# Two products of the scans, made as two products of 64 columns of weights where there was one of 128

## The reference, cut to what matters

```python
def step(S, inp):
    r_t, w_t, kk_t, a_t, v_t, k_t = inp
    sa = jnp.einsum('dbhij,dbhj->dbhi', S, -kk_t)
    S = S * w_t[..., None, :] + sa[..., None] * (kk_t * a_t)[..., None, :] + v_t[..., None] * k_t[..., None, :]
    return S, jnp.einsum('dbhij,dbhj->dbhi', S, r_t)
```

## Time and profile before

| | us |
|---|---|
| median of 3 runs | 3783.78 (3783.37 to 3785.37) |
| the profiled execution, its own time | 3779.27 |
| its span, first to last instruction | 3777.6 |
| scans stage, first to last chunk's work on PE | about 1058 to 1920 |
| one chunk in the middle of the stage | 24.0 |

### The profile page before, as it was taken

The page is one execution under the profiler, slowest core; times in us unless marked ns, Lnnn a source line. Parts: engine busy times, 40 slices in busy tenths (PEclk is TensorE's granted clock), DMA queues, the critical chain, the costliest instruction groups (busy, mean ns, idle before and its releaser), DMA issues. The chain is left out here.

```text
span 3777.6 us, 91654 instructions
## 1 busy us (share of the span) xinstructions
PE 3246.2 (86%) x37497; PEld 2921.0 (77%) x37497; DVE 2299.3 (61%) x4531; ACT 1613.9 (43%) x2876; POOL 852.2 (23%) x1205
## 2 busy tenths in 40 slices
PE   5879989998958999999948981699999999999990
PEld 2867776667658999999947770699999999999990
DVE  2555458985546777777757768355555555555542
ACT  2312665554633444444435640344444444444432
POOL 0100000000045666666622200111211111211001
PEclk8989999999878999999979985799999999999995
DMA  5444335654442444444366631555665555665536
GB/s 177 125 150 163 87 95 171 197 178 147 145 125 69 98 99 98 101 101 100 82 165 190 186 111 56 192 180 179 189 193 181 187 178 174 200 189 179 180 112 206
DMA packets 583699, 560.27 MB, mean 148 GB/s; under 512 B 212001, under 2 KB 527841, under 8 KB 582413
## 3 DMA queue, kind: packets, MB, share of 16 engines
q1 hardware_dynamic: 550768, 458.43, 40.9%
q0 software_dynamic: 32608, 97.26, 9.1%
HBM read 418.30 MB, written 137.27 MB: 147 GB/s over the span
## 5 line engine op out<-in xcount | busy, mean ns | idle before, releaser
L3114 DVE TENSOR_TENSOR exp_wlo<-exp_raw,exp_whi 128x2048 fp32r<-128x2048 f32 x192 | 440.5, 2294 | 373.8 <-ACT exp_whi L3067 373.8
L3067 ACT CAST exp_whi<-exp_raw 128x2048 fp32r<-128x2048 f32 x192 | 365.6, 1904 | 96.0 <-DMA exp_raw<-in_w_gate 96.0
L954 PE MATMUL mix_acc<-proj_hThi,mix_wlo 128*128 128x448 f32 (+3 forms) x920 | 366.2, 398 | 14.4 <-DVE mix_wlo L1279 14.4
L954 PE MATMUL mix_acc<-proj_hTlo,mix_whi 128*128 128x448 f32 (+3 forms) x920 | 342.7, 372 | 0.0
L954 PE MATMUL mix_acc<-proj_hThi,mix_whi 128*128 128x448 f32 (+3 forms) x920 | 342.3, 372 | 0.0
L3002 PE MATMUL exp_g<-exp_xThi,exp_wlo 128*128 128x272 f32 x1024 | 299.0, 292 | 8.6 <-DVE exp_xTlo L3118 7.4
L3002 PE MATMUL exp_o<-exp_hidhi,exp_wlo 128*128 128x272 f32 x1024 | 305.3, 298 | 0.0
L3002 PE MATMUL exp_g<-exp_xThi,exp_whi 128*128 128x272 f32 x1024 | 297.2, 290 | 0.0
L3002 PE MATMUL exp_o<-exp_hidhi,exp_whi 128*128 128x272 f32 x1024 | 296.7, 290 | 0.0
L3002 PE MATMUL exp_u<-exp_xThi,exp_wlo 128*128 128x272 f32 x1024 | 296.6, 290 | 0.0
L3002 PE MATMUL exp_u<-exp_xThi,exp_whi 128*128 128x272 f32 x1024 | 296.3, 289 | 0.0
(11 more groups left out here) (366 smaller groups left out, 8631.8 us busy)
## 6 DMA issues: line engine op xcount, KB each, us to landing
exp_raw<-in_w_gate SPq DMA_DIRECT2D x64, 1024.0 KB, 5.2
exp_raw<-in_w_up SPq DMA_DIRECT2D x64, 1024.0 KB, 5.2
exp_raw<-in_w_down SPq DMA_DIRECT2D x64, 1024.0 KB, 5.2
scn_plain<-rec SPq DMA_DIRECT2D x68, 384.0 KB, 3.6
rec<-mix_arena SPq DMA_DIRECT2D x24, 896.0 KB, 4.3
proj<-mix_out POOLq DMA_DIRECT2D x88, 224.0 KB, 2.6
scn_grc<-grec SPq DMA_DIRECT2D x136, 128.0 KB, 3.9
mix_arena<-in_w_ada SPq DMA_DIRECT2D x12, 1024.0 KB, 5.8
```

Source lines behind the costliest of these rows:

```text
L954: mm = pe.matmul(acc[n % ACCS][0:width, 0:tn], wt[:, k, 0:width], hT[hp][:, k, t0:t0 + tn], start=k == 0 and i == 0, stop=k == KD - 1 and ...
L3067: act.copy(w[k % RING][0][:, :, :], raw[k % RAW][:, :, :]).then_inc(hi_done[k % RING], 1)
L3114: dve.tensor_tensor(w[k % RING][1][:, :, :], raw[k % RAW][:, :, :], w[k % RING][0][:, :, :], ALU.subtract).then_inc(lo_done[k % RING], 1)
```

## The change

`read_out` and `keys_by_token` make each product of 128 columns of weights as two of 64 columns: the first takes columns 2C:3C and writes the low 64 partitions of the output, the second takes columns 3C:4C and writes the high 64. What is moved past them (the readings, or the identity `eye`) is the same for both. The same numbers land at the same places; the waits and semaphores are as before.

```diff
                         for h, p in enumerate(HALVES):
-                            mm = pe.matmul(cols(pRK[g][h], x, C), plain[u][p, j, 2 * C:4 * C], plain[u][p, j, C:2 * C], start=True, stop=True)
+                            for half, keys in ((LOW, slice(2 * C, 3 * C)), (HIGH, slice(3 * C, 4 * C))):
+                                mm = pe.matmul(cols(pRK[g][h], x, C)[half], plain[u][p, j, keys], plain[u][p, j, C:2 * C], start=True, stop=True)
...
                             for h, p in enumerate(HALVES):
-                                mm = pe.matmul(cols(pBK[g][h], x, C), plain[u][p, j, 2 * C:4 * C], eye[p], start=True, stop=True)
+                                for half, keys in ((LOW, slice(2 * C, 3 * C)), (HIGH, slice(3 * C, 4 * C))):
+                                    mm = pe.matmul(cols(pBK[g][h], x, C)[half], plain[u][p, j, keys], eye[p], start=True, stop=True)
```

## The result

The changed kernel takes 3792.39 us (median of 11 runs, 3782.22 to 3798.19), the kernel before 3782.54 (11 runs, 3776.01 to 3786.37). The ratio is 1.0025, with a 95% interval of 1.0014 to 1.0036: some 9.5 us slower, where 73 us less was forecast. The execution that was profiled is the changed kernel's quickest, 3782.22 us, so its trace shows less of the loss than the median has.

What follows compares the result with a forecast made beforehand. PE's own sequence was taken to bound each chunk: 3.55 us removed less 1.40 added gives 2.15 us, 73 us over 34 chunks, so 3783.8 - 73 = 3711 us, range 3704 to 3766.

Steps and rivals of the forecast that it cites:

- What bounds the kernel: In each chunk PE's own sequence sets the time, apart from one loop through DVE of 0.9 us.
- 2.15: Gain in us per chunk: 3.55 removed (products and borders) less 1.40 added; 73 us over 34 chunks.
- The price of the new products: The 48 products of 64 x 64 a chunk run four at once, 0.029 us each, 1.40 us; chance 0.47.
- 2.80 us: Rival: only two positions work at once, so the 48 products cost 2.80 us; 25 us faster, 3759; chance 0.32.
- The borders: Changes of form around the three changed groups cost 0.29 us each, 0.87 us a chunk, and would go to zero.
- The step that failed: Issue of 24 more products a chunk costs nothing, hidden while PE's queue is ahead of its array.
- 0.0583: Time in us of a 64 x 64 product before, the best rate of any group, read as two positions at once.
- DVE: It all but sets the stretch after the last changed group, which moves with that group, neither longer nor shorter.
- wait of 0.94 us: PE's one long wait for DVE, between 1519.77 and 1534.57 us, should stay.
- The rival on the other side: Switching output halves on the same rows costs 0.05 us a start, 4.00 us for 48; 15 us slower, 3799; chance 0.11.
- likeliest case: Four positions at once: 73 us faster, 3711 us, own range 3704 to 3728; chance 0.47.

Runs made afterwards that it cites:

- after_t: Kernel before with keys_by_token as one-pass transposes of 64 x 128 and read_out split into 64-column halves: 3760.52 us, ratio 0.9958.
- positions: Kernel before plus a stage ahead with PE alone on f32 products: 1600 round four positions 89.0 us, 1600 in two 93.6, 800 with 128 columns 89.3.
- experiments 8 and 9: Changed kernel and kernel before, each with most scan loads cut to one row from the fourth chunk: 3767.38 us (0.9966) and 3777.31 us (0.9993).

## Why the prediction was wrong

**What bounds the kernel** was half right. The claim was that PE's own sequence sets a chunk. PE's sequence is two things, the array and the supply of its instructions, and the kernel before was close to the limit of both. The instruction queue of 1300 to 1500 us, before and then changed:

```profile
q8 instruction: 44, 0.72, 1.6%
```

```profile
q8 instruction: 46, 0.75, 1.6%
```

That is a portion every 4.55 us before and every 4.35 now. In the changed kernel the waits in this stage follow each other at 256 instructions (125 or 126 product records, as many loads and the waits for semaphores), most of them 4.1 to 5.1 us apart (3.6 to 5.6, median 4.4), two or three in a row; then some 500 records, four portions, mostly pass in about 17 us, 4.2 to 4.3 each, without one. The supply, not the array, sets its chunk. Counted in the traces, a chunk of the kernel before is 5.26 portions and one of the changed kernel 5.64. At 4.35 us a portion, the pace of the changed kernel, a chunk before would need 22.9 of its 24.1 us: an estimate, by which about 1.2 us a chunk, not 2.15, was there to be had by anything that leaves the count alone. And the change didn't leave it alone. The pace is read off the changed kernel itself; what supports it is another kernel with another count: the chunks of `after_t`, 5.36 portions in 23.52 us, go at 4.39.

**The price of the new products** was nearly right: 1.40 us for 48. By starts, the steps behind those of 1962 and 1974 took 47.3 us in 29.5 chunks, 1.60 a chunk, where the old ones took 92.7 in 29.8, 3.11. Four positions do work at once, also where two share their rows. The rule of the Trainium skill's TensorE: Matmul & The Clock Gate (packing small matmuls), by which 2.80 us was worked out, isn't borne out here, and that of the Trainium skill's TensorEngine Tiling (Array Packing), Tiling Modes, is: 0.029 us a product in the bursts of `positions`. **The borders** vanished: the neighbour at 1509.60 is at 0.70.

**The step that failed** is "I cost the new issue of 24 more products at nothing: it is hidden as long as PE's queue is ahead of its array", and with it "the products would be paid at the rate of issue, which isn't slower than the 0.0583 seen". First, the queue isn't ahead: its supply is what the faster array runs into. Second, 0.0583 was no bound on the supply. It was seen where slower products, 64 x 128 at 0.112 us, stood between and let the portions catch up (64 of them last 7.2 us). Beside the traffic of the scans the waits that follow at one portion's distance are 4.4 us apart at the median, 0.069 us for an f32 product. The change took these slow products out and put more instructions in. 24 more products are 96 instructions, 0.375 of a portion, 1.6 us at 4.35. So of the 2.15 us a chunk that the array was to give, about 1.2 could be had at that pace, and the new instructions need 1.6. The chunk went from 24.09 to 24.52, with the four spells of half the clock in it.

**DVE** was judged rightly in that it wasn't what stopped the gain: its waits fell from 20.1 to 5.7 us. The prediction wanted its wait of 0.94 us, one of these, to stay. That they shrank because PE came later is likely, and wasn't tested. The reading of the trace of before that would have warned isn't in the one chunk of the earlier trace rows, which has no wait of PE for issue. It is in the list for 1100 to 1850: 8.1 us in 11 pieces, of which 3.8 are the piece behind `scn_SX` and 4.3 are short waits, each at a multiple of 256 instructions. In so full a stretch, an engine that waits for nothing visible was here the sign of a supply at its edge.

**The rival on the other side** had the right sign and nearly the right size (15 us slower, 9.5 measured), but by luck: its mechanism was a start of 0.05 us at each switch of halves, and in `positions` bursts round four positions run at 0.029 us. (A slip without weight: by its own terms the upper end of the likeliest case is 3730, not 3728.)

**Open.** That a portion waits for a transfer is shown by the count of instructions, the packets' size and their times. With PE alone its distance of 3.46 us is made up of 1.0 to 1.2 us until the next packet starts, 0.9 to 1.1 of the packet and 1.2 to 1.5 until its instructions are used; what the first and the last of these are spent on isn't shown. Of the 3.6 to 5.6 us in the scans, the traffic explains a part (experiments 8 and 9); the rest was not taken apart. What brings the clock to half behind some waits and not behind others as long isn't shown. The trace of the changed kernel is of its quickest run; of the runs that took 10 us more there is none.

## What to carry to other kernels

Before making matmuls shorter, count the engine's instructions and not only the array's time: f32 products of 64 x 64 are four instructions, and here 256 instructions came every 3.5 us at best with PE alone, and every 4.4 us beside the loads of the scans. Splitting a product over free positions paid where 64 products took longer than that (256 columns moved: twofold), and next to nothing where they took less (64 columns: 89.0 us against 93.6). The product after the split isn't the only one to look at: the waits fell on the neighbours. A form with fewer instructions, such as the one-pass transpose, gains on both counts: 29 us here.

## What the hardware showed that was not expected

With PE alone at work, a wait for issue falls at each 128th product record (256 instructions, 16.4 KB) round four positions, with 64 and with 96 columns moved, at a distance of 3.46 us, at times 3.74 or 4.0. The next packet of instructions started only after the wait was over. In the scans of the changed kernel every such wait between 1150 and 1850 us kept to multiples of 256 instructions, one more or less. Four positions of 64 x 64 in one array run, within a burst, at 0.029 us an f32 product of 64 columns moved, twice the rate of two (0.0583). The clock went to half for 3.4 us behind four waits of 1.75 to 1.94 us, in a stretch that was at the full clock in the kernel before.
